# A residual block with forgetting attention and gated DeltaNet: input projection by seven products ahead of the heads, and heads merged

## What is computed

```python
h = rms_norm(x, pre_mix_norm)                      # x: 1024 tokens x 1024, float32
proj = h @ w_in                                    # 1024 x 3600
fq, fk, fv, ff, gq, gk, gv, gb, ga, gz = split(proj)
# A: 8 heads of 64, causal softmax(q k^T / 8 + cum[q] - cum[k]) v, cum = cumsum(log_sigmoid(ff + bias)); rms_norm
# B: 4 heads of 128: q, k, v = silu(causal conv of 4 taps), q and k normalised; chunked delta rule:
t_inv = solve(eye + strict(k_beta @ k.T * decay)); u = t_inv @ v_beta; w = t_inv @ (k_beta * exp(gc))
v_new = u - w @ state; o = q_dec @ state + (q @ k.T * decay) @ v_new
state = state * g_last + k_dec.T @ v_new           # then rms_norm(o) * silu(gz)
x = x + rms_norm(concat(A, B) @ w_out, post_mix_norm)
x = x + rms_norm(square(relu(rms_norm(x) @ w_up)) @ w_down, post_mlp_norm)
```

## Time and profile before

| | |
|---|---|
| median of 3 runs | 1595.51 us (1594.02 to 1599.71) |
| profiled execution | 1597.14 us, its span 1595.3 us |
| TensorE busy | 1465.6 us, 92% |
| VectorE, ScalarE, GpSimd busy | 57%, 40%, 37% |
| DMA | 152.86 MB, mean 96 GB/s |
| granted TensorE clock, mean | 0.962 of full speed |

### The profile page before, as it was taken

One profiled execution on the slowest core, in us unless ns is written; L12 is line 12 of the kernel. 1 busy time (PEld: TensorE's weight loads), 2 busy tenths in 40 slices (PEclk: granted clock), 3 DMA queues, 4 the chain that ended last, 5 costly groups with the idle time before them and its releaser, 6 DMA issues.

```text
span 1595.3 us, 21734 instructions
## 1 busy us (share of the span) xinstructions
PE 1465.6 (92%) x7545; PEld 1206.0 (76%) x7545; DVE 913.0 (57%) x1490; ACT 644.6 (40%) x1347; POOL 596.9 (37%) x504
## 2 busy tenths in 40 slices
PE   4998999999999999987859988999999999999997
PEld 3877877788877877776748876888888786688885
DVE  5245346543565446545533578666666759844557
ACT  4334245532555235534622353233333343345443
POOL 1006234351425333363400145666666529631001
PEclk7999999999999999998779999999999999999999
DMA  5111101210101011101132333444444695233533
GB/s 180 40 53 40 27 14 41 69 27 14 53 14 55 27 28 41 44 24 54 40 117 95 122 102 113 158 149 148 146 145 146 238 357 187 88 99 95 203 99 139
DMA packets 135196, 152.86 MB, mean 96 GB/s; under 512 B 9453, under 2 KB 89757, under 8 KB 135081
## 3 DMA queue, kind: packets, MB, share of 16 engines
q1 hardware_dynamic: 135080, 151.39, 29.2%
HBM read 109.37 MB, written 41.99 MB: 95 GB/s over the span
## 4 chain that ended last, share of the span: by engine, by line
PE 73%; DVE 14%; issue 6%; ACT 3%; DMA 1%; POOL 1%; SPq 1%; DVEq 0%; ACTq 0%; POOLq 0%
PE ps L2092 7%; PE ps L2333 6%; PE ps L2332 6%; PE ps L2331 6%; PE ps L2035 6%; PE ps L2036 5%; PE ps L2037 5%; PE ps L2344 5%; PE ps L2346 4%; PE ps L2345 4%; PE ps L2197 4%; DVE db_lo L1762 3%; DVE da_lo L1760 3%; PE ps L2097 2%; PE ps L2285 2%
## 5 line engine op out<-in xcount | busy, mean ns | idle before, releaser
L2035 PE MATMUL ps<-big_hi,w_hi 128*128 128x512 f32 x464 | 215.8, 465 | 0.0
L2036 PE MATMUL ps<-big_lo,w_hi 128*128 128x512 f32 x464 | 188.0, 405 | 0.0
L2344 PE MATMUL ps<-db_hi,da_hi 128*128 128x512 f32 x448 | 177.5, 396 | 10.8 <-DVE db_lo L1762 10.8
L2037 PE MATMUL ps<-big_hi,w_lo 128*128 128x512 f32 x464 | 186.2, 401 | 0.0
L2346 PE MATMUL ps<-db_hi,da_lo 128*128 128x512 f32 x448 | 174.6, 390 | 0.0
L2345 PE MATMUL ps<-db_lo,da_hi 128*128 128x512 f32 x448 | 174.5, 389 | 0.0
L1760 DVE TENSOR_TENSOR da_lo<-a_raw,da_hi 128x512 fp32r<-128x512 f32 x112 | 104.4, 932 | 100.3 <-ACT da_hi L1305 100.3
L1305 ACT ACTIVATE da_hi<-a_raw 128x512 fp32r<-128x512 f32 x112 | 70.7, 631 | 173.6 <-PE ps L2346 153.2
L2331 PE MATMUL ps<-bt_hi,ring_hi 128*128 128x512 f32 x320 | 126.9, 396 | 5.6 <-DVE ring_lo L1682 5.6
L2333 PE MATMUL ps<-bt_hi,ring_lo 128*128 128x512 f32 x320 | 127.8, 399 | 0.0
L2332 PE MATMUL ps<-bt_lo,ring_hi 128*128 128x512 f32 x320 | 127.1, 397 | 0.0
(11 more groups left out here) (287 smaller groups left out, 3394.5 us busy)
## 6 DMA issues: line engine op xcount, KB each, us to landing
a_raw<-act_dram SPq DMA_DIRECT2D x112, 256.0 KB, 2.6
act_dram<-s_act SPq DMA_DIRECT2D x64, 256.0 KB, 2.0
wd<-in_w_down_dram SPq DMA_DIRECT2D x15, 1024.0 KB, 6.7
w_raw<-in_w_in_dram SPq DMA_DIRECT2D x28, 512.0 KB, 3.9
act_dram<-c SPq DMA_DIRECT2D x48, 256.0 KB, 4.9
w_raw<-in_w_up_dram SPq DMA_DIRECT2D x18, 512.0 KB, 4.7
w_bot<-in_w_up_dram SPq DMA_DIRECT2D x16, 512.0 KB, 5.8
x_in<-in_x_dram SPq DMA_DIRECT2D x8, 512.0 KB, 6.4
```

The costliest lines, as they stand in the source:

```text
L2035: nc.tensor.matmul(acc, w_hi[s][:, k, :], rhs_hi, start=(k == 0), stop=False)
L2036: nc.tensor.matmul(acc, w_hi[s][:, k, :], rhs_lo, start=False, stop=False)
L2037: last = nc.tensor.matmul(acc, w_lo[s][:, k, :], rhs_hi, start=False, stop=(k == KT - 1))
L2344: nc.tensor.matmul(acc, da_hi[s][:, cols], db_hi[s][:, :], start=start, stop=False, skip_group_check=True)
```

## The change

**Projection.** `w_in` is taken in 14 pairs of blocks of the same kind of two neighbouring heads (`PAIR_KINDS`), all ahead of any head. A pair is one 256 x 1024 times 1024 x 1024 product in 2 x 2 quarters, by seven products of 4 x 3 matmuls (`in_up`). For that the transposed x is kept as `i_ba_hi/lo` (left half of the tokens) and as five combinations `i_bt_hi/lo`, split ahead; GpSimd forms four sums of weights per pair (`s_part`). The gates' right half is put together from three terms. Results go to `o_top`, `o_bot`; the conv's first tap is ScalarE's (`tap0`), the others VectorE's (12 operations per pair with a convolution, in the turns of the next pair); silu or scale follows, and the rows are stored to `proj_dram`.

**Heads.** No loop is left. One list `ORDER` merges, in five phases, the fills of head p, 14 attention tiles (10 in the last phase, two of which only drain) and the scan of head p-1. Rows are loaded from `proj_dram` as they are needed; operands of the scan have two sets of buffers. Fills have three banks in place of six. The query copies are gone, as the queries are loaded twice, 64 rows each.

**Outputs.** The normalised outputs stay in SBUF (`mixed_half`) and TensorE transposes them from there; `mixed` is neither stored nor loaded. The output weights are split in the last phase, by ScalarE and GpSimd.

```diff
-NFILL_BANKS = 6
+NFILL_BANKS = 3
+FOX_PARTS = 4
+FOX_IN_PHASE = (14, 14, 14, 14, 10)
+ORDER = [("fill", 0, "fv", g, 0) for g in range(2)]
+for _p in range(GDN_HEADS + 1):
+    _first = sum(FOX_IN_PHASE[:_p])
+    _fills = [("fill", _p) + s for s in HEAD_PREP] if _p < GDN_HEADS else []
+    if _p + 1 < GDN_HEADS:
+        _fills += [("fill", _p + 1, "fv", g, 0) for g in range(2)]
+    ORDER += spread(_fills, fox_parts(_first, FOX_IN_PHASE[_p]), scan_parts(_p - 1) if _p else [])
...
+            k_hi(0)
+            for item in ORDER:
...
+                    elif n == 1:
+                        if i < NFT:
+                            fox_exps(i)
+                        if 1 <= i <= NFT:
+                            p_chunk(i - 1, 0)
+                    elif n == 2:
+                        if 1 <= i <= NFT and FOX_TILES[i - 1][2] >= 4:
+                            p_chunk(i - 1, 1)
+                        if i >= 2:
+                            fox_square(i - 2)
...
+                for k in range(HK):
+                    nc.tensor.matmul(acc, i_ring_hi[r][:, k, :], b_hi[:, k, :], start=(first and k == 0), stop=False, skip_group_check=True)
+                    nc.tensor.matmul(acc, i_ring_hi[r][:, k, :], b_lo[:, k, :], start=False, stop=False, skip_group_check=True)
+                    last = nc.tensor.matmul(acc, i_ring_lo[r][:, k, :], b_hi[:, k, :], start=False, stop=(k == HK - 1), skip_group_check=True)
...
+            for item in ORDER:
...
+                    if n == 0 and i < NFT:
+                        scores(i)
+                    elif 1 <= i <= NFT:
+                        qb = FOX_TILES[i - 1][2]
+                        if n == 1:
+                            turn(i - 1, 0)
+                        elif n == 2:
+                            if qb >= 4:
+                                turn(i - 1, 1)
+                            times_v(i - 1, 0)
+                        elif n == 3 and qb >= 4:
+                            times_v(i - 1, 1)
...
-                pe.wait_ge(w_loaded[t % 2], 16 * (SLOT_LOADS[t % 2] - NT // 2 + t // 2 + 1))
+                pe.wait_ge(mixed_ready, len(NORMS) - (1 if t < HT else 0))
...
+            def k_hi(n):
+                act.wait_ge(kk_loaded, 32 * (n + 1))
...
+                elif n == 0:
+                    for s in range(2):
+                        act.wait_ge(proj_stored[s], stores_of(NPAIR - 2 + s))
```

More of the change, by code:

```diff
@@ new lines, with last_chunk, spread, fox_parts @@
+FOX_PARTS = 4
+FOX_IN_PHASE = (14, 14, 14, 14, 10)
+def last_chunk(i):
+    return FOX_CHUNK[(i, FOX_TILES[i][2] // 4)]
+def spread(*lists):
+    placed = [((n + 0.5) / len(items), m, item) for m, items in enumerate(lists) for n, item in enumerate(items)]
+    return [item for _, _, item in sorted(placed, key=lambda p: p[:2])]
+def fox_parts(first, count):
+    out = []
+    for i in range(first, first + count):
+        out += [("fox", i, n) for n in range(FOX_PARTS)]
+        if i % 16 == 2 and i > 16:
+            out.append(("mean", ("fox", i // 16 - 1)))
+        if i % 16 == 3 and i > 16:
+            out.append(("norm", ("fox", i // 16 - 1)))
+    return out
@@ new lines, in scan_parts @@
+def scan_parts(h):
+    out = [("mean", ("gdn", h - 1, 1))] if h else []
+    for c in range(NCHUNK):
+        out += [("scan", h, c, 0), ("scan", h, c, 1)]
+        if c == 0 and h:
+            out.append(("norm", ("gdn", h - 1, 1)))
+        if c == 5:
+            out.append(("mean", ("gdn", h, 0)))
+        if c == 6:
+            out.append(("norm", ("gdn", h, 0)))
+    return out
+ORDER = [("fill", 0, "fv", g, 0) for g in range(2)]
[5 more added lines that the diff above has]
+    ORDER += spread(_fills, fox_parts(_first, FOX_IN_PHASE[_p]), scan_parts(_p - 1) if _p else [])
@@ L142 @@
+_last = [("gdn", GDN_HEADS - 1, 1), ("fox", GDN_HEADS - 1)]
+ORDER += [("mean", t) for t in _last] + [("norm", t) for t in _last]
+FILLS = [o[1:] for o in ORDER if o[0] == "fill" and o[2] not in NOT_FILLS]
 FILL = numbered(FILLS)
@@ L174 @@
 ACT_PREP, DVE_PREP, POOL_PREP = numbered(_act), numbered(_dve), numbered(_pool)
[L175 to L202, removed]
[L203 to L216 removed]
+TAILS = [o[1] for o in ORDER if o[0] == "mean"]
@@ new lines, in turn_gates @@
+            def turn_gates(half):
+                if half == 0:
+                    pe.wait_ge(gate_dve, 5)
+                    pe.wait_ge(gate_act, 5)
+                    pe.wait_ge(conv_ready, 1)
+                else:
+                    pe.wait_ge(gates_copied, 2)
+                    pe.wait_ge(gates_exp, 2)
+                for t in range(HT):
+                    cols = slice((half * HT + t) * P, (half * HT + t + 1) * P)
+                    last = nc.tensor.transpose(turned_ps[:, t * P:(t + 1) * P], gate_rows[:, cols], ident)
+                last.then_inc(gate_turned, 1)
@@ new lines, in wait_copied, with turn @@
+            def wait_copied(n):
+                pe.wait_ge(pt_act if n % 2 == 0 else pt_dve, n // 2 + 1)
+            def turn(i, c):
+                n = FOX_CHUNK[(i, c)]
+                if c == 0:
+                    pe.wait_ge(fox_exp, i + 1)
+                if n >= 1:
+                    wait_copied(n - 1)
+                for kb in range(4 * c, min(4 * c + 4, FOX_TILES[i][2] + 1)):
+                    last = nc.tensor.transpose(fox_t[:, (kb - 4 * c) * P:(kb - 4 * c + 1) * P], probs[i % 2][:, kb * P:(kb + 1) * P], ident)
+                last.then_inc(fox_turned, 1)
```

2246 lines of the change are left out of this document (1303 added, 943 removed), and 4 rows, old and new, of tables (HEAD_PREP, PREP_FILLS).

## The result

The changed kernel takes **1642.15 us** (median, 1639.64 to 1644.23) against 1594.86 us for the kernel before in the same comparison: a ratio of 1.0292 [1.0276, 1.0307], slower by 2.9%. I had forecast 1568 us and a gain. The profiled execution took 1642.74 us for a span of 1640.9 us; its parts are read against the sum of 803 us.

The account below looks back on a forecast made before the run. TensorE was taken to bound three heads, hand-overs between engines the last. Projection 322, hand-over 9 and 6, merged stage 454, clock 4 and end 8 gave 803 us where 830.1 was, so 1568 us; range 1515 to 1622.

Parts of the forecast that it names:

- the sum of 803 us: Time up to the output projection's first transposes: 322 + 9 + 6 + 454 + 4 + 8, where 830.1 was.
- part 5: Merged stage of preparation, attention and scan: 454 us (404 to 500), and 4 us for the clock.
- the 4 us for the clock: Merged stage: added for dips of TensorE's clock where it idles.
- parts 1 to 3: Projection by seven products, its start and the convolution beside it: pair 0's product 6 near 57 us, end 322 (312 to 338).
- that rival: Projection: VectorE bounds the pairs with taps, 20 us in place of 4; 1584 us, chance 0.13.
- part 1's 64 us: Projection: TensorE's work saved by 156 fewer and denser matmuls, about 350 us down to 286.
- part 4: Hand-over through DRAM from projection to heads: 9 us (7 to 12), and 6 more during first norms (0 to 8).
- 45 + 32 + 17 = 94: Merged stage, TensorE's idle us: 45 for copies behind exp, 32 for preparations' own stalls, 17 in the last phase.
- my floor: Merged stage: TensorE's work for four heads, 360 us.
- the third rival: Merged stage: hand-overs, three fill banks and the lower clock make it 500 us, deciding from 481; 1614 us, chance 0.15.
- part 6: End of the heads, before the output projection: 8 us of TensorE waiting (6 to 10), where 14.4 was.
- no overlap at all: Merged stage, high bound: four times 125 us from the last head's times before, 500 us.

Follow-up runs that it names:

- The early loads: Changed kernel with the first head's loads, the forgetting heads' v first, ahead of the last pairs' stores on the DMA queue: 1634.21 us.
- the last one: Changed kernel with four edits of order, two in VectorE's list, tiles as 16, 15, 15, 15, 5 and nine preparation items ahead of the first tile: 1548.1 us.
- the three single edits with a gain: Changed kernel with one edit each: copy ahead of exp 1612.93 us, first head's loads ahead of last stores 1634.21, state cleared early 1632.77.
- the copy first: Changed kernel with ScalarE's copy of the previous tile's turned probabilities (first chunk) ahead of the next tile's exp: 1612.93 us.
- a shorter last phase: Changed kernel with the four edits of order, and attention tiles as 16, 15, 15, 15, 5 in place of 14, 14, 14, 14, 10: 1572.62 us.
- the four edits: Changed kernel with copy ahead of exp, GpSimd's mask later, state cleared early, and first head's loads ahead of the last stores: 1596.22 us.

## Why the prediction was wrong

The sign was wrong, by one term of part 5 above all: the 4 us for the clock. The surcharge was 54 us; with these 50 us away the span would be 1591 us, level with the kernel before. Point by point:

- *Projection, parts 1 to 3.* Right in kind, somewhat late. Product 6 of pair 0 starts at 62.4 us (forecast 57; the bound was 62), behind gate products that run without a wait from the late start of the ring (5.7 us of waiting for `i_ring_lo_B` at 39.7). The last product ends at 338.8 us, forecast 322 (312 to 338). Of the 17 us, 5 are the start; the stretch takes 277 us where 264 are the matmuls, and TensorE waits for VectorE only 8.4 us in it; the rest is a clock of 0.98. A tap takes 0.75 us with GpSimd still and 1.23 us beside it (means of 51 and of 20 taps in this stretch), so operations do get longer as part 3 held, but VectorE is busy for only 186.6 of the 277 us: the taps do not bound the pairs, and that rival is out. The 156 matmuls fewer are there, 36 us at 0.2315 us each. That all of part 1's 64 us were saved isn't shown: with the surcharge of the slow stretches taken out on both sides, TensorE's busy time falls by 41 us (from 1422.8 to 1381.4, my estimate from the two traces).
- *Hand-over, part 4.* Mis-sized: 20.9 us against 9 (7 to 12). I had named some ten issues of 0.4 us ahead of v_fox, 4 us, but the sum went by the 8.3 us of one store and one load and had only 0.7 us above them. The issues are eight and take 6 us (343.10 to 349.17), the load takes 10.4 us with the DMA engines busy for 0.86 of the stretch, and the last pair's convolved rows are stored only behind silu, at 341.3. The early loads show that taking this away brings 8 us, since the split of k stands behind the same stores.
- *Idle time in the merged stage, part 5.* Nearly right in size, in part by luck: 102.5 us where 45 + 32 + 17 = 94 stood. ScalarE's copy of the probabilities is TensorE's first releaser, as said, with 30.3 + 8.4 us against 45. Not in the sum: VectorE's copies (26.9 us) and the cleared state (11.6 us), both held up in VectorE's list. What stands against the 32 us of the preparations' own stalls is less than that: the rows of the fills come to some 24 us.
- *The clock, part 5: the step that failed.* I added 4 us "for such dips". TensorE's busy time is 402.5 us where 360 + 4 was forecast. 109 of it is at the lower level, so half of that, 54 us, is surcharge, and the work itself is 348 us, 12 less than my floor. The earlier trace rows had the size: 58.9 busy in 71 us brought 0.78 (28 of these 58.9 us at the lower level, of 60 in all four heads' 645). I took it for a property of the last head, and had the low clock for the whole stage only in the third rival, at 0.15. But 94 us of idle time in pieces of 1 to 5 us is just such a stage, all along: each wait was priced at its own length. From the changed kernel to the last one 96 us of span went with 57 us of waits, 1.7 times; for the three single edits with a gain the ratio lies between 1.3 (the loads) and 2.0 (the copy first), and it is 2.4 against the kernel without a merge. So 1.7 is a mean of this stage, not the price of every wait. The Trainium skill puts the penalty of the warm-up at under 1% of a typical kernel's span (TensorE: Matmul & The Clock Gate, What's actually happening); here the clock fell again and again, 16 stretches in one stage, and 54 of 1641 us are 3.3%: for this kernel the measurement decides.
- *End of the heads, part 6, and the rest.* 10.4 us of waiting against 8 (6 to 10); GpSimd's list had 2.3 us of the output weights' low part ahead of the powers, which the chain had left out. From the first transposes (875.3 us) to the end 765.6 us, against 765.2 carried over: nothing in what is unchanged depends on the order before it.
- *The sum.* Against 1568: start and projection 17, hand-over 12, merged stage 505 against 464 (454, 6 and 4), 41, the end 2: 72 of the 73 us.
- *The rivals.* The third came true in its signs: three of the four phases with fills take 113 to 117 us, and the stage is above the 481 us from which it decides, with the low clock as its price. But its "three fill banks" do not show (the rows of fills waiting for copies are 6.9 us and less; no run has six banks again), and its price was lucky: "no overlap at all", which I put at 500 us, is 662. I had treated it as the far end of the merged stage, when overlap was worth more, and hand-overs cost more, than I thought, and the two errors cancelled in it.

Open: why a shorter last phase is worth 24 us was not taken apart. Against the four edits' its trace has TensorE's busy time 8.6 us lower, and its waits for VectorE's copies 10 us and for ScalarE's 9 us lower (32.2 to 22.2, and 14.2 to 5.3).

## What to carry to other kernels

When engines run fixed lists, look for each instruction that waits for another engine's short step (a power of four columns, an exp) and ask what stands behind it that needs none of it; such edits of order were worth 86 us here (1642 to 1557, 8 of them by a DMA queue), more than the 64 us of TensorE's work that part 1 had put on the change of algorithm. Price a wait of TensorE at its length and the slow stretch behind it, from a row of the same kernel that has waits of that size. And price "no overlap" with the order that will be in place, not with that of the kernel before.

## What the runs showed of the hardware

The busy time of TensorE is not a fixed cost of its work: the same matmuls took 1409.6 to 1541.1 us, by order alone, with 38 to 275 us of it at the lower of its two clocks. Useless products in its waits gave back some 11 to 13 of the 31 us that they took, and the rest lay in the waits, so that they cost half a microsecond in all. A tap of VectorE with two SBUF inputs took 0.75 us with GpSimd still and 1.23 us beside it.
